# Fewer experts in fixed order, a wide step earlier, and two reorderings at the start of a mixture-of-experts stage

## The reference, cut to what matters

```python
scores = sigmoid(t @ w_router)                 # 256 tokens x 64 experts
sel = scores + router_bias                     # group-limited top 8 of 64
...
combine = sum(one_hot(ei, 64) * w)             # weights of the chosen experts
gu = einsum('td,edf->etf', t, w_expert_gate_up)    # 64 x (1024 x 512)
g, u = split(gu, 2)
act = silu(g) * u * combine.T[:, :, None]
routed = einsum('etf,efd->td', act, w_expert_down) # 64 x (256 x 1024)
```

## Time and profile before

| what | us |
| --- | --- |
| median of 3 runs | 814.75 (811.74 to 814.78) |
| profiled execution, its own time | 813.52 |
| its span in the profile | 811.6 |
| PE busy in the span | 777.0 |
| DVE busy | 374.0 |
| ACT busy | 239.3 |

### The profile page before, as it was taken

One profiled execution on the slowest core, in us unless ns is written; L12 is line 12 of the kernel. 1 busy time (PEld: TensorE's weight loads), 2 busy tenths in 40 slices (PEclk: granted clock), 3 DMA queues, 4 the chain that ended last, 5 costly groups with the idle time before them and its releaser, 6 DMA issues.

```text
span 811.6 us, 13310 instructions
## 1 busy us (share of the span) xinstructions
PE 777.0 (96%) x5438; PEld 525.2 (65%) x5438; DVE 374.0 (46%) x761; ACT 239.3 (29%) x426; POOL 21.9 (3%) x22
## 2 busy tenths in 40 slices
PE   5999999999999999999999999799999999999985
PEld 3689897999999999955455355254454745455222
DVE  1267999889998667463222222121221131122114
ACT  3354747354364444131112112111111111111002
POOL 1000010100100100200000000000000000000000
PEclk9999999999999999999999999999999999999998
DMA  9999798533534299799899999999999999999996
GB/s 354 408 398 349 281 404 296 198 104 111 201 108 167 94 336 420 301 418 409 359 396 425 427 427 426 426 427 427 426 425 426 427 426 427 426 426 428 426 424 250
DMA packets 69102, 284.73 MB, mean 351 GB/s; under 512 B 5520, under 2 KB 7856, under 8 KB 44208
## 3 DMA queue, kind: packets, MB, share of 16 engines
q1 hardware_dynamic: 68608, 282.67, 86.5%
q10 hardware_dynamic: 432, 1.18, 0.4%
HBM read 280.67 MB, written 3.16 MB: 350 GB/s over the span
## 4 chain that ended last, share of the span: by engine, by line
PE 74%; DMA 12%; SPq 6%; DVE 4%; issue 2%; ACT 1%; POOL 0%; DVEq 0%; POOLq 0%; ACTq 0%
PE bank L2203 16%; PE bank L2256 8%; DMA chunk<-in_w_expert_gate_up 7%; SPq L636 6%; PE bank L1768 6%; PE bank L1770 5%; PE bank L1773 5%; PE bank L2083 4%; PE bank L2111 4%; DMA chunk<-in_w_expert_down 3%; PE bank L1717 3%; PE bank L1812 3%; PE bank L1790 2%; PE bank L1794 2%; PE bank L1792 2%; PE bank L1846 2%
## 5 line engine op out<-in xcount | busy, mean ns | idle before, releaser
L2203 PE MATMUL bank<-chunk,xg 128*64 128x512 f32 (+2 forms) x1024 | 196.7, 602 | 6.5 <-DMA chunk<-in_w_expert_gate_up 6.3
L2203 PEld LDWEIGHTS bank<-chunk,xg 128*64 128x64 f32 (+2 forms) x1024 | 61.9, 127 | 134.7 <-issue 118.9
L2256 PE MATMUL bank<-chunk,act_t 128*64 128x512 f32 (+2 forms) x480 | 97.3, 612 | 7.7 <-ACT act_t L1007 3.9
L1568 DVE SCALAR_TENSOR_TENSOR act_r<-bank,w_slot,sil 128x256 f32<-128x256 f32 x26 | 12.6, 484 | 168.2 <-ACT sil L1005 168.2
L1580 DVE TENSOR_TENSOR y_lo<-bank,y_hi 128x512 fp32r<-128x512 f32 x52 | 36.0, 692 | 74.4 <-ACT y_hi L1018 74.4
L2256 PEld LDWEIGHTS bank<-chunk,act_t 128*64 128x64 f32 (+2 forms) x480 | 30.1, 129 | 55.2 <-issue 54.5
L1005 ACT ACTIVATE sil<-bank 128x256 f32<-128x256 f32 x26 | 10.0, 384 | 183.4 <-PE bank L2203 183.4
L1116 DVE TENSOR_TENSOR ring_lo<-ring,ring_hi 128x1024 fp32r<-128x1024 f32 x44 | 52.8, 1217 | 15.6 <-ACT ring_hi L786 15.5
L1018 ACT ACTIVATE y_hi<-bank 128x512 fp32r<-128x512 f32 x52 | 31.0, 597 | 98.1 <-PE bank L2256 94.8
L1177 DVE SCALAR_TENSOR_TENSOR conv<-upad,dw,conv 128x256 f32<-128x256 f32 x120 | 52.8, 514 | 0.0
L786 ACT ACTIVATE ring_hi<-ring 128x1024 fp32r<-128x1024 f32 x44 | 44.6, 1054 | 24.5 <-PE bank L1794 19.0
(11 more groups left out here) (318 smaller groups left out, 1166.6 us busy)
## 6 DMA issues: line engine op xcount, KB each, us to landing
chunk<-in_w_expert_gate_up SPq DMA_DIRECT2D x128, 1024.0 KB, 25.4
chunk<-in_w_expert_down SPq DMA_DIRECT2D x62, 1024.0 KB, 26.0
ring<-in_w_in SPq DMA_DIRECT2D x15, 2048.0 KB, 10.5
ring<-in_w_ada SPq DMA_DIRECT2D x12, 2048.0 KB, 10.2
ring<-in_w_proj_hgrn SPq DMA_DIRECT2D x2, 2048.0 KB, 7.6
ring<-in_w_out SPq DMA_DIRECT2D x2, 2048.0 KB, 11.3
ring<-in_w_proj_conv SPq DMA_DIRECT2D x1, 2048.0 KB, 8.2
chunk<-in_w_shared_gate_up SPq DMA_DIRECT2D x2, 1024.0 KB, 27.1
```

Of the source, the lines that this page charges most:

```text
L2203: ins = mm(bank[2 + b][row:row + width, :], xg[:, k, c:c + width], w[:, k % 4, :], start=(k == 0), stop=(k == KD - 1))
L2256: ins = mm(out[row:row + width, :], act_t[:, c, row:row + width], w[:, c, h * 512:(h + 1) * 512], start=(c == 0), stop=(c == 1))
```

## The change

1. `FIXED` goes from 8 to 6: three fixed steps (chunks 0 to 17). `RANKED` is 58 and `MIDDLE` 25. The list of steps is the same but for two that change places: step 3 becomes a ranked `FOUR` (chunks 18 to 29), step 4 a `TWO` (30 to 35). From step 5 on widths and chunk numbers are as before. The single waits of chunks 19 and 20 move into the ranked loop, and chunks 18 to 20, now ranked, wait for `order_done`.
2. The down product of step 1 moves into the gather for steps 2 and 3, between its block 1 and its block 2, and the split of its result by ACT and DVE with it (`DOWN_AMID_GATHER = (1,)`).
   The function `gathered_next` below is ACT's; DVE's is changed in the same way around its blocks 1 and 3.
3. In the first gather the two passes with the low parts are done for blocks 0 and 1 first, then for blocks 2 and 3.

```diff
-FIXED, WIDE, MIDDLE, NARROW = 8, 3, 23, 30
+FIXED, WIDE, MIDDLE, NARROW = 6, 3, 25, 30
-STEPS = [TWO] * FIXED_STEPS + [FOUR, TWO, TWO, FOUR, TWO, TWO, FOUR, ONE, TWO, ONE, FOUR, ONE, TWO, TWO, FOUR, TWO, TWO, FOUR, TWO, TWO, MIX, FOUR]
+STEPS = [TWO] * FIXED_STEPS + [FOUR, TWO, TWO, TWO, FOUR, TWO, TWO, FOUR, ONE, TWO, ONE, FOUR, ONE, TWO, TWO, FOUR, TWO, TWO, FOUR, TWO, TWO, MIX, FOUR]
+DOWN_AMID_GATHER = (1,)
...
-                        freed(number - NCHUNK)
+                        if number == 19:
+                            sp.wait_ge(s_x1_kept, 16)
+                            sp.wait_ge(x1_sq, 5)
+                            sp.wait_ge(g_done, 5)
+                        if number == 20:
+                            filled(sp, "hr", 0)
+                        if number >= NCHUNK:
+                            freed(number - NCHUNK)
...
             def gathered_next(i, amid=None):
                 gathered(0, i * 2 + 3)
+                if amid is not None:
+                    amid()
                 gathered(2, i * 2 + 4)
...
-            evacuated(pe, "hr", 1)
-            first_gather(2, 0, h_lo)
-            evacuated(pe, "hr", 3)
-            first_gather(3, 1, h_lo)
+            for parts in (range(0, 2), range(2, 4)):
+                evacuated(pe, "hr", 1)
+                first_gather(2, 0, h_lo, parts)
+                evacuated(pe, "hr", 3)
+                first_gather(3, 1, h_lo, parts)
...
                 gather(1)
+                if amid is not None:
+                    amid()
                 pe.wait_ge(ga_evac, i * 2 + 3)
                 gather(2)
...
+                if n in DOWN_AMID_GATHER:
+                    gather_next(i, lambda: down(n))
                     turn_step(n + 1)
                     continue
```

More of the change, by code:

```diff
@@ L1007, in gate, with gathered_next @@
                 nc.scalar.activation(act_t[:, :, :].rearrange("p c n -> p (c n)"), bank[2 + b][:, 0:2 * P], ACT.Copy).then_inc(t_evac, 1)
-            def gathered_next(i):
+            def gathered_next(i, amid=None):
                 gathered(0, i * 2 + 3)
+                if amid is not None:
+                    amid()
                 gathered(2, i * 2 + 4)
@@ L1048, in _ @@
                     gathered_next(n // 2)
+                    continue
+                if n in DOWN_AMID_GATHER:
+                    gathered_next(n // 2, lambda: result_hi(n % 2, n))
                     continue
@@ L1611, in _ @@
                         extra_one_hots(RANKED)
+                elif n in DOWN_AMID_GATHER:
+                    gathered_next(i, lambda: result_lo(b, n))
+                    turned(n + 1)
+                    continue
                 elif i + 1 < NIT:
@@ L2124, in _, with first_gather @@
             ins.then_inc(cnt_ready, 1)
-            def first_gather(n, s, src):
-                for part in range(4):
+            def first_gather(n, s, src, parts=range(4)):
+                for part in parts:
                     for c in range(2):
@@ L2178, in shared_down, with gather_next @@
                 ins.then_inc(shared_done, 1)
-            def gather_next(i):
+            def gather_next(i, amid=None):
                 pe.wait_ge(built, i + 3)
@@ L2317, in _ @@
                     continue
+                if n in DOWN_AMID_GATHER:
+                    gather_next(i, lambda: down(n))
+                    turn_step(n + 1)
+                    continue
                 if b and i + 1 < NIT:
```

## The result

The changed kernel is slower by a little: 815.08 us median of 14 runs (813.19 to 816.53) against 813.87 us of 14 runs of the kernel before (811.61 to 814.78). The ratio is 1.0017, 95% interval 1.0009 to 1.0025, that is +0.7 to +2.0 us where -0.6 was forecast. That lies within the 0.5% that the forecast called "no change", but on the other side of it. The profiled execution took 814.91 us with a span of 813.0; before it was 813.52 and 811.6.

The account below looks back on a forecast made before the run. DMA was taken to bound the kernel. A new 4.5 us loss minus old losses of 3.75 and 1.40, reorderings about 0, gave -0.6 us: 813.5 us, between 812.9 and 814.1, range 810.5 to 816.5.

Parts of the forecast that it names:

- (b): Chunk 18 now waits for the order, so the DMA queue is dry from 352.5 to 357.0: a new 4.5 us loss.
- restart of 1.6 us: DMA flow returns 1.6 us after an issue into an empty queue, taken from chunk 31; upper bound 2.1 us.
- the tail behind the last bytes: Work after the last weight chunk lands, near 786 us: claimed fixed, so no term in the sum.
- The bound, and what moves it: DMA, full at 426 GB/s from 425 us, sets the end; only empty-queue losses before 425 us move the time.
- (a): Step 3 as a FOUR sends chunk 43 10 us earlier, removing the 1.40 us loss at 417 to 424.
- the fetch limps after the order: Rival: number reads over 2.46 us a chunk, or chunks 18 to 21 each restarting an empty queue: +5.8 us, 4%.
- the spacing of 1.1: Chunks 19 and 20 follow chunk 18 at 1.1 us each on SP, taken from the pair at 368.04.
- the ledger of the dips: New loss at 352 minus the old losses at 385 and 417: 4.5 - 3.75 - 1.40 = -0.65 us.
- My second count: Counting bytes from 357.0 puts chunk 43 at 419.0, including 0.5 us for a lower rate, against 419.6 before.
- (c): The queue lasts to 389.0, so the 3.75 us loss at 385 goes if chunk 31 is issued before 387.4.
- The reorderings at 0: Down product amid the gather: 0 by itself; first gather by halves: 0 to -0.2 us on PE, 0 for DMA.
- cut 2.4 us off the loss at 385: Claim for moving step 1's down product into its gather without the six fixed experts: 2.4 us less lost at 385.

Follow-up runs that it names:

- the run with the late order: Changed kernel with SP also waiting, behind the order, for a later DVE result before fetching chunk 18: 817.87 us, 1.0049 of the kernel before.
- the run with the hoisted waits: Changed kernel, order matmul between the first gather's halves, waits of chunks 19 and 20 ahead of the order wait: 813.40 us, 0.9997 of the kernel before.
- added products: 12 small unused products in PE's last wait; ratios to the kernel before: on that kernel 0.9993, changed 1.0013, hoisted waits 0.9984, eight experts with both reorderings 0.9998.
- the early order alone: Changed kernel, order matmul between the first gather's halves, e_row written before DVE's first copy: 813.69 us, 0.9997 of the kernel before.

## Why the prediction was wrong

Two steps failed. In (b) the flow was taken to be whole behind one restart of 1.6 us, and the chunks behind it were priced at 0; they cost another 0.8 us. That takes the forecast of -0.6 to about zero. And the tail behind the last bytes was taken as fixed; in the profiles it was 0.7 us longer with six experts, by the slowest DMA engine. What makes the timed runs 1.2 us slower beyond the first of these stays open in part. That the time still fell into the range owes more to the width of the range than to the account.

**The bound, and what moves it: right.** DMA sets the end from 425 us on at 426 GB/s, and the run with the late order shows that the end follows the fetch of chunk 18, by 2.5 to 3.3 us for 3.3. What was wrong is the addition that "the tail behind it is fixed"; see the ledger below.

**(a), the dips at 385 and 417 go: right.** Chunk 43 went at 407.15 and both windows are full.

**(b), a new dip of 4.5 us from 352.5: right in place, one term short.** The window 352 to 358 lost 6 x (1 - 98/426) = 4.6 us, beside the 4.5 that follow from the restart of 1.6 us. What I left out is the next row: 6 x (1 - 371/426) = 0.8 us from 358 to 364. I costed one restart of the queue, for chunk 18, and took it that the flow is whole from there on. But chunk 19 was issued 1.65 us behind it, and a second loss follows. The first 8 us behind the issue of chunk 18 show it, in the changed kernel, in the run with the hoisted waits and in that with the late order, where the spacing is 1.65, 1.16 and 1.26 us:

```profile
355.03:363.03 8.00, 7.76 (x44) 3.27 (x41) 3.28 (x23) 0.82 (x3) 0.00 (x0) 1.00 0.84 292
354.73:362.73 8.00, 8.00 (x42) 3.02 (x38) 3.20 (x21) 1.65 (x3) 0.00 (x0) 1.00 0.85 331
357.93:365.93 8.00, 7.75 (x44) 3.53 (x42) 3.31 (x15) 1.56 (x4) 0.00 (x0) 1.00 0.85 325
```

These are losses of 8 x (1 - 292/426) = 2.5, 1.8 and 1.9 us. The five profiles with the wide spacing have 2.4 to 2.7 us, the three with a narrow one 1.8 to 1.9, and chunk 31 in the kernel before 1.6. So the restart itself was about right, and the wide spacing behind it cost 0.5 to 0.9 us more. I had even written this down as a rival ("the fetch limps after the order") and dismissed it, because it asked for a spacing above 2.46 us. That condition was wrong: 1.65 us is already too much. Where the limit lies between 1.26 and 1.65 us, and why it lies so far below a chunk's own 2.46, no run shows. And the spacing of 1.1 was taken from a pair at another place, where nothing stands between the two but the number read.

On the Trainium skill's 0.6 us to the first byte (DMA: Bandwidth & Descriptors, section Latency and other measured facts) the dip would by estimate have been 3.5 us, which this window doesn't bear out.

With the second loss the ledger of the dips reads 4.6 + 0.8 - 3.75 - 1.40 = +0.25 in place of -0.6. It leaves out what the kernel before lost between its dips, 30 x (1 - 419/426) = 0.5 us from 355 to 385. My second count carried that over to the changed kernel, which has 426 GB/s from 364 to 384. With it the ledger is about -0.25, and the whole stretch says -0.4. So this term takes the forecast from -0.6 to about zero, and no further.

**(c), chunk 31 in time: right**, at 383.95.

**The reorderings at 0: right**, 1.0003 and 0.9995. But the sentence that the down product amid the gather would by itself "cut 2.4 us off the loss at 385" was misleading: it does, and most of it is lost again at 390, 402 and 417, since chunks 33 and 43 wait for times that PE sets.

**What the ledger doesn't hold: the tail isn't fixed.** The flow hardly separates six experts from eight. From 345 to 425 us the four profiles with eight experts and no added products moved 395, 399, 398 and 399 GB/s, the three with six and the old order 397, 398 and 398; over the 75 us behind the start of the gather, which isn't at the same moment in all of them, the six lost 0.2 us more on average. Yet the medians lie 0.9 to 1.5 us apart. Counted from the start of the first gather, the last product starts at 437.3 to 437.6 us in those three profiles, and at 436.4 to 436.9 in the four: some 0.8 us. The mean landing of the chunk that it waits for differs by only 0.1 of them, and in the first pair it is even 0.25 us earlier in the changed kernel. The other 0.7 us are how far the slowest of the 16 DMA engines is behind that mean (below). On top of this comes, in the first pair, 1.1 us of half clock in the last product, which by the runs with the added products doesn't carry over to the timed difference. So the prediction's step from the last bytes to the end failed in the profiles: it priced the bytes, took the rest as constant, and the rest moved by more than the forecast. Whether the slowest engine is also what costs 1.2 us in the timed runs stays open. I have no run that moves it alone, and the pair with the added products speaks against it: there the slowest engine is 2.2 us behind in both profiles and the last product starts only 0.3 us later, but the medians are 1.2 us apart.

**The uncertainty.** A sum of a few tenths from losses of 5 us each needs every term to some 0.1 us, and I took the restart from one sample and the spacing from another place, and gave the tail no term at all. The range held the time; the sign was not known well enough to be given as a forecast with only 5% on the side of "slower".

## What to carry to other kernels

Where a transfer queue runs dry, look at when each chunk behind the dry spell is released, and by whom: a dry spell that is shortened comes back at the next release that has a fixed time on another engine. Behind a restart count the spacing of the first two transfers too; here 1.65 us between them cost 0.5 to 0.9 us more than 1.16 or 1.26. Add up the flow of the whole stretch and not of the dips alone. And give up work that can be fetched ahead of a data-dependent order only if the order's path has been shortened first: here 0.7 us off that path was, within the uncertainty, worth as much as the whole change cost. A step shape that is cheap at the end of a kernel, since another engine is the bound there, has to be costed again before it is moved.

## What the runs showed that I had not expected

- **A step of mixed tile widths takes more than twice as long on TensorE.** At a granted clock of 1.00, 48 matmuls of one 64-column tile and two of 32 take 15.90 us, 32 of two 64-column tiles and 64 of four 32-column ones 7.07 each. The down product of a mix takes 7.55 us for 3.65.
- **A chunk lands with its slowest DMA engine, and these drift apart.** From the landing records of the trace, the last of a chunk's 16 increments minus their mean, for the landing that ends at about 786 us: 1.6 us in the kernel before, 2.5 and 2.6 in the two profiles of the changed one, 1.7 with the halves alone, 2.9 with eight experts, both reorderings and the products. It steps up at single moments; the instruction fetches (45 packets of 16 KB on the page's queue q8) come one at a time as well. That the one causes the other is a guess from the times, and no run tests it.
- **SP's issue path has its own small costs.** An expert's number and the issue take about 1.1 us. Another 0.5 us turn up once at the start of the ranked chunks: between 18 and 19 in the changed kernel (1.65 us), ahead of 18 with the waits hoisted (1.53 us from `e_row` to the issue, where it was 1.02 with the early order alone). The three waits aren't its cause by themselves, as with the late order they stand in their place and the spacing is 1.26. What is, stays open.
